# Expert down weights read in 16 KB pieces, and small parameters loaded as rows

## The chip, the cores and the metric

The kernel runs on one core of a Trainium2 chip. The metric is the device time of one execution in microseconds (us), as the median of several runs.

## The reference

The input is `x`, 256 tokens of 1024 float32 numbers. Two layers of the first block run in turn, then a final norm, then two layers of a second block:

```python
for l in range(2):
    x = x + hybrid_mixer(rmsnorm(x, norm_mix[l]), w_in[l], ...)          # attention and convolution
    x = x + hierarchical_moe(rmsnorm(x, norm_ffn[l]), router..., w_gate[l], w_up[l], w_down[l])
x = rmsnorm(x, norm_final)
# second block: swiglu (d_ff 2816), pool mixer, swiglu | swiglu, sparse attention, swiglu
def expert_block(xb, e):
    return (silu(xb @ w_gate[e]) * (xb @ w_up[e])) @ w_down[e]           # 32 experts per layer
```

An expert's gate and up weights are 1024 x 512 and its down weights 512 x 1024 float32, so each of the three is 2 MiB (2.097 MB), and the two layers read 64 experts x 3 x 2.097 MB = 403 MB of them. The small parameters are norm gains (vectors of 1024 or 512), convolution taps, attention sinks, router weights and biases, and the position tables of the sparse attention.

## The kernel before, in words

The stages run in the order mix0, moe0, mix1, moe1, final, ffn00, pool, ffn01, ffn10, nsa, ffn11. Each engine has an order written out by hand and waits on semaphores for the others.

**Weights.** All large weights are loaded by DMAs that the SP queue issues, each 2 MiB or less, into a ring of six slots (`ring`); in a MoE stage three more slots lie in `work` (`slot_of`), nine in all. A load is issued when the matmuls that used the slot's last content are done. The expert loads go pair by pair in the order gate, gate, up, up, down, down (`PAIR`, `moe_loads`; the issuing line is L530). The first nine loads of a MoE stage (`fill`) go out while the mixer before it still computes; the 87 that are left (`refill`) wait for PE to finish a gate, an up or a down product of an earlier pair. Gate and up weights are laid out so that partition `p` holds the rows `8p` to `8p+7`, 16 KB that lie together in memory; the down weights so that partition `p` holds the rows `p`, `p+128`, `p+256`, `p+384`, four pieces of 4 KB (`expert_src`).

**A pair of experts** (`one_pair` of the tensor engine): gate and up products (L905), the turn of the hidden activations `EB.h` by four 128 x 128 transposes (L943), the gather of the next pair's tokens (L892), the down product (L917), and the combination of the pair before (L926).

**Small parameters.** GpSimd issues all of them (`par`, L655), 7 for mix0 under one semaphore (`mix_param_loaded`) and 30 for the rest (`param_loaded`). The vectors are loaded in turned form, so that each 4-byte number is a piece of its own: element `k*128+p` goes to partition `p`. SP issues `x`, the constants table `cst` (identity and others), and the first two loads of `w_in`, then waits for the 7 parameter loads before it goes on. ScalarE and VectorE wait for the same 7 before they scale the turned `x` (L1395, L1826). PE turns `x` (L737), multiplies by `w_in` (L753 and L763) and later by `w_out` (L814). The mixer of layer 1 runs the same code.

Of the kernel before, what the change touches and what calls it, by code (L numbers as in the profile page):

```python
# [10 lines left out]
ALU = mybir.AluOpType  # L11
# [3 lines left out]
P = 128  # L15
SEQ, D = 256, 1024
TT = SEQ // P
KT = D // P
# [110 lines left out]
def build(nc, a, out, stages):  # L129
    ctx = ExitStack()  # L130
    with ctx:
# [30 lines left out]
        gT = sb("gT", [P, 10, KT])  # L162
        cw = sb("cw", [P, 2, 3, 4])
        gaT = sb("gaT", [P, 2, 4])
        gcT = sb("gcT", [P, 2, 4])
# [5 lines left out]
        cpos = sb("cpos", [P, 2, 16])  # L171
# [37 lines left out]
        S.mix_param_loaded = sem("mix_param_loaded")  # L209
# [73 lines left out]
        def expert_sems(tag, slots=RING):  # L283
# [17 lines left out]
            s.step = sem(f"step_{tag}")  # L301
            s.base_added = sem(f"base_added_{tag}")
# [4 lines left out]
        OV = {l: expert_sems(f"more{l}") for l in range(2) if f"moe{l}" in stages}  # L307

# [148 lines left out]
        FFN_GAIN = {"ffn00": 2, "ffn01": 3, "ffn10": 4, "ffn11": 6}  # L457
# [6 lines left out]
        MIX_PARAMS, PARAMS = 16 * 7, 16 * (8 + 6 + 2 + 6 + 1 + 2 + 1 + 4)  # L464
# [5 lines left out]
        def _(sp):  # L470
# [177 lines left out]
        N_PARAMS = [0, 0]  # L648

        @block.gpsimd  # L650
        def _(pool):
            w = Follow()

            def par(dst, src, first=False):
                pool.dma_start(dst, src).then_inc(S.mix_param_loaded if first else S.param_loaded, 16)  # L655
                N_PARAMS[0 if first else 1] += 16

            with nc.allow_non_contiguous_dma(reason="small parameters, transposed"):
                g2 = a["norm_gains_2"]
                def mixer_params(l):  # L660
                    for t in range(3):
                        par(cw[:, l, t, :], a["conv_w"][l, t].rearrange("(c p) -> p c", p=P), l == 0)
                    par(sink[:, l, :], a["attn_sink"][l].partition_broadcast(P), l == 0)
                    par(gcT[:, l, :], a["norm_conv_out"][l].rearrange("(c p) -> p c", p=P), l == 0)
                    par(gaT[:, l, :], a["norm_attn_out"][l].rearrange("(c p) -> p c", p=P), l == 0)
# [9 lines left out]
                mixer_params(1)  # L675
                par(gT[:, 1, :], a["norm_mix"][1].rearrange("(k p) -> p k", p=P))
                par(gT[:, 5, :], g2[1, 2].rearrange("(k p) -> p k", p=P))
                for n, src in ((2, g2[0, 0]), (3, g2[0, 4]), (4, g2[1, 0]), (6, g2[1, 4]), (7, g2[0, 2])):
                    par(gT[:, n, :], src.rearrange("(k p) -> p k", p=P))
# [3 lines left out]
                for s, name in enumerate(("nsa_cmp_pos_k_2", "nsa_cmp_pos_v_2")):  # L683
                    for r in range(2):
                        par(cpos[r * DH:(r + 1) * DH, s, :],
                            a[name][0].rearrange("(j r) d -> r d j", r=2)[r])
# [1718 lines left out]
```

## Time and profile before

| | us |
|---|---|
| median of 3 runs | 2221.74 |
| lowest and highest run | 2219.32, 2222.49 |
| the profiled execution's own time | 2221.96 |
| its span, first to last instruction | 2220.1 |
| PE busy in it | 2109.5 (95%) |
| VectorE busy | 775.1 (35%) |
| ScalarE busy | 631.8 (28%) |
| GpSimd busy | 35.7 (2%) |
| SP queue's packets, as a share of 16 DMA engines | 68.1% |

PE, PEld, DVE, ACT, POOL and SP are the tensor engine's matmuls and weight loads, VectorE, ScalarE, GpSimd and SyncE; a q behind a name is that engine's queue of instructions.

### The profile page before, as it was taken

How to read it: one execution, taken by the hardware profiler on the slowest of the kernel's cores; microseconds unless marked ns; L12 is line 12 of the kernel's file. 1: busy time of each engine (PE TensorE's matmuls, PEld its weight loads, DVE VectorE, ACT ScalarE, POOL GpSimd, SP SyncE). 2: the span in 40 equal slices, each digit the busy share in tenths (PEclk: the TensorE clock that was granted, in tenths of full speed). 3: DMA queues.
4: the chain of work that ended last, by engine and by line, in shares of the span. 5: the costliest groups of instructions: out<-in, count | busy, mean ns of one | idle time of the engine just before them, and what ended most of it. 6: DMA issues, size and time to landing. Idle time of an engine off the chain costs nothing.

```text
span 2220.1 us, 28261 instructions
## 1 busy us (share of the span) xinstructions
PE 2109.5 (95%) x11946; PEld 1427.5 (64%) x11946; DVE 775.1 (35%) x1151; ACT 631.8 (28%) x932; POOL 35.7 (2%) x53
## 2 busy tenths in 40 slices
PE   6999999999989999999998999899999999999998
PEld 4764444444467544444443999689989994667997
DVE  1431111111124311111112655465565542475555
ACT  1311111111123111111112433343343332373333
POOL 5000000000000000000000000000000000000000
PEclk9989999999999999999999999999999999999999
DMA  9449999999973599999999743464464454504530
GB/s 268 186 190 394 420 420 423 423 423 421 413 270 139 201 424 421 422 421 422 421 422 410 290 148 110 161 247 151 170 223 158 160 194 141 190 1 152 208 112 21
DMA packets 142467, 599.05 MB, mean 270 GB/s; under 512 B 6913, under 2 KB 22337, under 8 KB 126002
## 3 DMA queue, kind: packets, MB, share of 16 engines
q1 hardware_dynamic: 139730, 592.01, 68.1%
q0 software_dynamic: 2656, 5.86, 1.1%
q8 instruction: 63, 1.03, 0.2%
q14 instruction: 18, 0.15, 0.0%
HBM read 596.80 MB, written 1.05 MB: 269 GB/s over the span
## 4 chain that ended last, share of the span: by engine, by line
PE 76%; DMA 14%; DVE 4%; SPq 4%; ACT 1%; issue 1%; DVEq 0%; ACTq 0%
PE PS L1047 21%; PE PS L905 13%; PE PS L1061 10%; PE PS L917 6%; DMA work<-in_w_expert_up 5%; DMA ring<-in_w_expert_up 5%; PE PS L763 4%; SPq L530 4%; PE PS L892 3%; PE PS L1134 3%; PE PS L814 3%; PE PS L1034 2%; PE PS L753 2%; PE PS L926 2%; DMA work<-in_w_expert_down 1%; PE PS L1287 1%
## 5 line engine op out<-in xcount | busy, mean ns | idle before, releaser
L905 PE MATMUL PS<-ring,xs 128*64 128x512 f32 x1408 | 381.9, 598 | 16.1 <-DMA ring<-in_w_expert_up 16.1
L1315 ACT ACTIVATE split<-ring 128x2048 fp32r<-128x2048 f32 x132 | 253.2, 1921 | 425.9 <-PE PS L1047 268.0
L1792 DVE TENSOR_TENSOR split<-ring,split 128x2048 fp32r<-128x2048 f32 x132 | 302.4, 2293 | 178.0 <-ACT split L1315 172.9
L1047 PE MATMUL PS<-hT_high,split 128*128 128x256 f32 x2560 | 329.1, 281 | 0.0
L1047 PEld LDWEIGHTS PS<-hT_high,split 128*128 128x128 f32 x2560 | 316.5, 189 | 2.8
L905 PEld LDWEIGHTS PS<-ring,xs 128*64 128x64 f32 x1408 | 124.0, 138 | 219.7 <-issue 205.4
L1061 PE MATMUL PS<-split,ffn_hid 128*128 128x512 f32 x1056 | 246.9, 390 | 0.0
L905 PE MATMUL PS<-work,xs 128*64 128x512 f32 x640 | 217.2, 615 | 15.8 <-DMA work<-in_w_expert_up 15.8
L1061 PEld LDWEIGHTS PS<-split,ffn_hid 128*128 128x128 f32 x1056 | 195.5, 188 | 39.0
L1047 PE MATMUL PS<-hT_low,split 128*128 128x256 f32 x1280 | 178.3, 282 | 0.0
L1984 DVE TENSOR_TENSOR work<-PS,work 128x512 f32<-128x512 f32 x32 | 22.1, 691 | 410.9 <-PE PS L905 410.9
L1047 PEld LDWEIGHTS PS<-hT_low,split 128*128 128x128 f32 x1280 | 163.6, 189 | 0.0
L1990 DVE SCALAR_TENSOR_TENSOR y_low<-PS,work,y_high 128x512 fp32r<-128x512 f32 x64 | 48.0, 750 | 308.1 <-ACT y_high L1489 308.1
L905 PEld LDWEIGHTS PS<-work,xs 128*64 128x64 f32 x640 | 70.5, 142 | 111.3 <-issue 111.1
L917 PE MATMUL PS<-ring,work 128*64 128x512 f32 x640 | 141.7, 595 | 0.0
L1315 ACT ACTIVATE work<-PS 128x512 f32<-128x512 f32 (+1 forms) x65 | 40.0, 619 | 341.1 <-PE PS L943 295.9
L892 PE MATMUL PS<-work,hp 128*128 128x128 f32 x1024 | 124.2, 281 | 3.1 <-DVE work L1965 3.1
L892 PEld LDWEIGHTS PS<-work,hp 128*128 128x128 f32 x1024 | 121.4, 198 | 3.9 <-issue 3.9
L1489 ACT ACTIVATE y_high<-PS,work 128x512 fp32r<-128x512 f32 x64 | 44.0, 687 | 187.2 <-PE PS L917 187.2
L917 PEld LDWEIGHTS PS<-ring,work 128*64 128x64 f32 x640 | 44.2, 137 | 82.4 <-issue 80.0
L763 PE MATMUL PS<-hT,ring 128*128 128x256 f32 x384 | 87.3, 383 | 0.0
L917 PE MATMUL PS<-work 128*64 128x512 f32 x384 | 85.0, 595 | 0.9 <-DMA work<-in_w_expert_down 0.9
(287 smaller groups left out, 1851.2 us busy)
## 6 DMA issues: line engine op xcount, KB each, us to landing
ring<-in_w_expert_gate SPq DMA_DIRECT2D x44, 2048.0 KB, 24.4
ring<-in_w_expert_up SPq DMA_DIRECT2D x44, 2048.0 KB, 26.8
ring<-in_w_expert_down SPq DMA_DIRECT2D x40, 2048.0 KB, 31.5
work<-in_w_expert_down SPq DMA_DIRECT2D x24, 2048.0 KB, 30.2
work<-in_w_expert_gate SPq DMA_DIRECT2D x20, 2048.0 KB, 23.9
work<-in_w_expert_up SPq DMA_DIRECT2D x20, 2048.0 KB, 26.8
ring<-in_ffn_w_gate SPq DMA_DIRECT2D x20, 2048.0 KB, 8.6
ring<-in_ffn_w_up SPq DMA_DIRECT2D x20, 2048.0 KB, 8.9
```

The lines of the kernel that those rows point to most:

```text
L530: sp.dma_start(slot_of(r, 4 if which == "down" else KT), expert_src(l, 2 * pair + e, which)) \
L763: last = pe.matmul(PS[:, bank, (c % 2) * SEQ:(c % 2 + 1) * SEQ], wv[:, k, c * P:(c + 1) * P], hT[:, k, :], start=(k == 0), stop=(k == KT - 1))
L814: last = pe.matmul(PS[:, bank + h, :], src[:, c, t * P:(t + 1) * P], wv[:, c, h * 512:(h + 1) * 512], start=(c == 0), stop=(c == 3))
L892: last = pe.matmul(PS[:, 6 + b, (k % 4) * P:(k % 4 + 1) * P], hp[:, t, k * P:(k + 1) * P], EB.OH[:, t, :], start=(t == 0), stop=(t == 1))
L905: last = pe.matmul(PS[e * CAP:(e + 1) * CAP, bank, :], xs[:, k, e * CAP:(e + 1) * CAP], slot_of(slots[e], KT)[:, k, :], start=(k == 0), st ...
L917: last = pe.matmul(PS[e * CAP:(e + 1) * CAP, 6 + c, :], EB.hT[:, k, e * CAP:(e + 1) * CAP], slot_of(slots[e], 4)[:, k, c * 512:(c + 1) * 512],
L1047: last = pe.matmul(PS[:, bank, ft * SEQ:(ft + 1) * SEQ], split_cols(b, kind, part)[:, k, ft * P:(ft + 1) * P], hx[:, k, :], start=(n_ == 0 ...
L1061: last = pe.matmul(PS[:, 2 * t + c, :], ffn_hid[:, b % 2, hpart, ft, t * P:(t + 1) * P], wv[:, ft, c * 512:(c + 1) * 512], start=(b == 0 a ...
L1134: last = pe.matmul(PS[:, banks[t], offs[t]:offs[t] + width], hT[:, k, t * P:(t + 1) * P], wv[:, k, :], start=(k == 0), stop=(k == KT - 1))
L1315: return act.activation(o, i, ACT.Copy)
L1792: v.tensor_tensor(at[:, 1], src, at[:, 0], ALU.subtract).then_inc(S.ffn_low, 1)
L1990: v.scalar_tensor_tensor(y_low[:, c, :], PS[:, 6 + c, :], EB.gs[:, 0:1], y_high[:, c, :], ALU.mult, ALU.subtract).then_inc(s.y_made, 1)
```

## The change

1. `expert_src` lays the down weights out as `(p f) n -> p f n`: partition `p` reads the rows `4p` to `4p+3`, 16 KB in one piece. The hidden activations are turned to match: transpose `k` reads every fourth column of `EB.h`, from column `k`.
2. The gains, the convolution taps and the position tables are read as 152 rows of 128 numbers by 8 DMAs that ScalarE issues before its first stage, into a corner of `work` (`param_rows`). PE turns them by two transposes, and VectorE copies the 152 columns into one tile (`params`), of which `gT`, `cw`, `gaT`, `gcT`, `cpos` are now views.
3. GpSimd first loads one sink table, waits until the first two products with `w_in` are done (`projected` at 3), and only then issues its other 12 parameter loads.
4. SP loads `cst` before `x`, and its wait for the small parameters between the second and third load of `w_in` is gone.
5. Inside the MoE code VectorE counts its own steps with one semaphore where it had several, the numbering of the gains changes, and the branch for an expert with more than 64 tokens, which this input does not take, counts differently.

```diff
+        params = sb("params", [P, 152])
+        gT = params[:, 0:80].rearrange("p (n k) -> p n k", k=KT)
+        cw = params[:, 80:104].rearrange("p (l t c) -> p l t c", l=2, t=3)
...
+        param_rows = work[:, WORK - 2 * P:WORK].rearrange("p (a q) -> p a q", a=2)
...
                 if which == "down":
-                    return a["w_expert_down"][l, e].rearrange("(f p) n -> p f n", p=P)
+                    return a["w_expert_down"][l, e].rearrange("(p f) n -> p f n", f=4)
...
                 for lo, hi, k in ((0, 512, 2), (512, 768, 1), (1280, 1792, 2), (1792, 2304, 2), (768, 1280, 2)):
-                    if n[0] == 2:
-
-                        sp.wait_ge(S.mix_param_loaded, MIX_PARAMS)
                     wide(wi, lo, hi, S.projected, k, "(k p) n -> p k n")
...
+            sp.dma_start(cst[:, :], a["consts"]).then_inc(S.const_loaded, 16)
             sp.dma_start(x[:, :, :], a["x"][0].rearrange("(t p) d -> p t d", p=P)).then_inc(S.x_loaded, 16)
-            sp.dma_start(cst[:, :], a["consts"]).then_inc(S.const_loaded, 16)
...
-            with nc.allow_non_contiguous_dma(reason="small parameters, transposed"):
...
-                par(gT[:, 0, :], a["norm_mix"][0].rearrange("(k p) -> p k", p=P), True)
-                mixer_params(0)
+            pool.dma_start(sink[:, 0, :], a["attn_sink"][0].partition_broadcast(P)).then_inc(S.sink_loaded, 16)
+            pool.wait_ge(S.projected, 3)
+            with nc.allow_non_contiguous_dma(reason="small parameters"):
                 for l in range(2):
                     par(wr[:, l, :, 0:NG], a["w_router_group"][l].rearrange("(k p) n -> p k n", k=KT))
                     par(wr[:, l, :, NG:], a["w_router_expert"][l].rearrange("(k p) n -> p k n", k=KT))
-                    par(gT[:, 8 + l, :], a["norm_ffn"][l].rearrange("(k p) -> p k", p=P))
                     par(rbias[:, l, 0:NG], a["b_router_group"][l].partition_broadcast(P))
                     par(rbias[:, l, NG:], a["b_router_expert"][l].partition_broadcast(P))
...
             pool.wait_ge(S.param_loaded, PARAMS)
+            pool.wait_ge(S.rows_taken, 1)
...
                 transpose_x(f"mix{l}", 4)
+                pe.wait_ge(S.rows_taken, 1)
                 project(512, (0, 1), first=True)
...
                     for k in range(4):
-                        last = pe.transpose(PS[:, 4, k * P:(k + 1) * P], EB.h[:, k * P:(k + 1) * P], ident)
+                        last = pe.transpose(PS[:, 4, k * P:(k + 1) * P],
+                                            EB.h.rearrange("p (q k) -> p k q", k=4)[:, k, :], ident)
...
             pe.wait_ge(S.const_loaded, w.to(S.const_loaded, 16))
+            pe.wait_ge(S.rows_loaded, ROWS)
+            pe.transpose(PS[:, 0, 0:104], param_rows[0:104, 0, :], ident[0:104, 0:104])
+            pe.transpose(PS[:, 0, 104:152], param_rows[0:48, 1, :], ident[0:48, 0:48]).then_inc(S.rows_turned, 1)
             pe.wait_ge(S.set_up, w.to(S.set_up, 2))
...
                 if l == 0:
-                    act.wait_ge(S.mix_param_loaded, MIX_PARAMS)
+                    act.wait_ge(S.rows_taken, 1)
...
+            g2 = a["norm_gains_2"]
+            for dst, src in ((param_rows[0:16, 0, :], a["norm_mix"].rearrange("l (k p) -> (l k) p", p=P)),
+                             (param_rows[16:64, 0, :], g2.rearrange("i (j b) (k p) -> b (i j) k p", b=2, p=P)[0]),
+                             (param_rows[64:80, 0, :], a["norm_ffn"].rearrange("l (k p) -> (l k) p", p=P)),
+                             (param_rows[80:104, 0, :], a["conv_w"].rearrange("l t (c p) -> (l t c) p", p=P)),
+                             (param_rows[0:8, 1, :], a["norm_attn_out"].rearrange("l (c p) -> (l c) p", p=P)),
+                             (param_rows[8:16, 1, :], a["norm_conv_out"].rearrange("l (c p) -> (l c) p", p=P)),
+                             (param_rows[16:32, 1, :], a["nsa_cmp_pos_k_2"][0].rearrange("(j r) d -> j (r d)", r=2)),
+                             (param_rows[32:48, 1, :], a["nsa_cmp_pos_v_2"][0].rearrange("(j r) d -> j (r d)", r=2))):
+                act.dma_start(dst, src).then_inc(S.rows_loaded, 16)
...
                 if l == 0:
-                    v.wait_ge(S.mix_param_loaded, MIX_PARAMS)
+                    v.wait_ge(S.sink_loaded, 16)
...
             v.memset(epsb[:, :], EPS).then_inc(S.set_up, 1)
-            v.wait_ge(S.x_loaded, w.to(S.x_loaded, 16))
             v.wait_ge(S.const_loaded, w.to(S.const_loaded, 16))
             v.tensor_copy(ident_r[:, :], ident)
             v.tensor_copy(causal_r[:, :], const("causal")).then_inc(S.set_up, 1)
+            v.wait_ge(S.rows_turned, w.to(S.rows_turned))
+            v.tensor_copy(params[:, :], PS[:, 0, 0:152]).then_inc(S.rows_taken, 1)
+            v.wait_ge(S.rows_taken, w.to(S.rows_taken))
+            v.wait_ge(S.x_loaded, w.to(S.x_loaded, 16))
```

## Rows read from the trace of the kernel before

**Rows 1.** The page: busy tenths and GB/s of 40 slices of 55.5 us.

```profile
DMA  9449999999973599999999743464464454504530
GB/s 268 186 190 394 420 420 423 423 423 421 413 270 139 201 424 421 422 421 422 421 422 410 290 148 110 161 247 151 170 223 158 160 194 141 190 1 152 208 112 21
```

**Rows 2.** The chain that ended last: start us, us, what.

```profile
1.75 19.79 DMA ring<-in_w_in
...
140.00 5.35 PE PS L994 x24
...
214.37 13.73 PE PS L905 x64
...
241.41 13.73 PE PS L905 x64
...
446.02 7.11 PE PS L905 x32
...
505.75 8.49 PE PS L905 x32
...
574.12 31.09 DMA work<-in_w_expert_down
...
1193.54 21.57 DMA ring<-in_ffn_w_up
```

**Rows 3.** Stretches: us, busy us (instructions) per engine, granted clock, DMA share, GB/s.

```profile
397.00:412.00 15.00, 15.00 (x84) 6.91 (x84) 2.48 (x7) 3.85 (x5) 0.00 (x0) 1.00 1.01 428
...
416.50:423.50 7.00, 7.00 (x26) 2.58 (x24) 0.00 (x0) 0.00 (x0) 0.00 (x0) 0.76 1.02 407
...
810.00:1180.00 370.00, 354.89 (x1832) 163.59 (x1830) 49.91 (x117) 65.11 (x91) 0.00 (x0) 0.99 1.01 422
```

**Rows 4.** Packets of 397 to 412 us, then of 416.5 to 423.5 us.

```profile
DMA packets 440, 6.42 MB, mean 428 GB/s; under 512 B 48, under 2 KB 48, under 8 KB 48
...
DMA packets 712, 2.85 MB, mean 407 GB/s; under 512 B 16, under 2 KB 16, under 8 KB 712
```

**Rows 5.** First 50 us in order: start us, us, instruction [idle before <-releaser].

```profile
0.76 0.44 SPq L613 DMA_DIRECT2D x<-in_x  x1
...
2.04 0.20 ACT L1353 ACTIVATE small<-epsb 128x1 f32<-128x1 f32 x1
...
8.50 3.65 PE L737 MATMUL PS<-cst,x 128*128 128x128 f32 x16 [8.50 <-DVE causal_r L2356]
...
12.50 1.57 ACT L1395 ACTIVATE hT<-PS,gT 128x256 f32<-128x256 f32 x4 [2.85 <-DMA gaT<-in_norm_attn_out]
...
21.59 23.75 PE L753 MATMUL PS<-ring,hT 128*128 128x512 f32 x64 [9.44 <-DMA ring<-in_w_in]
```

**Rows 6.** DMA traffic and issues of the first 30 us; KB each, us to landing.

```profile
GB/s 0 0 87 153 360 360 382 413 370 199 180 143 191 237 292 226 251 259 153 241 292 200 183 167 115 179 245 215 260 249 185 132 138 144 189 243 210 202 179 189
DMA packets 4102, 6.31 MB, mean 210 GB/s; under 512 B 896, under 2 KB 1984, under 8 KB 4102
...
x<-in_x SPq DMA_DIRECT2D x1, 1024.0 KB, 5.2
...
gaT<-in_norm_attn_out POOLq DMA_DIRECT2D x2, 2.0 KB, 6.7
```

**Rows 7.** In order of time, layer 0 ends and layer 1 begins.

```profile
603.14 0.60 PE L943 MATMUL PS<-cst,work 128*128 128x128 f32 x4
...
605.35 7.09 PE L917 MATMUL PS<-work 128*64 128x512 f32 x32 [0.47 <-DMA work<-in_w_expert_down]
...
621.21 3.64 PE L737 MATMUL PS<-cst,x 128*128 128x128 f32 x16 [6.00 <-issue]
...
624.69 20.88 PE L753 MATMUL PS<-ring,hT 128*128 128x512 f32 x64
```

**Rows 8.** Stretches behind x's transposes, columns as in rows 3.

```profile
624.80:631.80 7.00, 7.00 (x18) 3.17 (x18) 2.01 (x11) 1.87 (x5) 0.00 (x0) 1.00 1.04 394
...
1451.00:1458.00 7.00, 7.00 (x49) 7.00 (x49) 6.89 (x17) 3.62 (x6) 0.00 (x0) 0.78 0.85 340
```

More of the change, by code:

```diff
@@ L208, in build @@
         S.x_loaded = sem("x_loaded")
-        S.mix_param_loaded = sem("mix_param_loaded")
+        S.rows_loaded = sem("rows_loaded")
+        S.rows_turned = sem("rows_turned")
+        S.rows_taken = sem("rows_taken")
+        S.sink_loaded = sem("sink_loaded")
         S.param_loaded = sem("param_loaded")
@@ L307, in build @@
         OV = {l: expert_sems(f"more{l}") for l in range(2) if f"moe{l}" in stages}
+        for l in OV:
+            OV[l].step = sem(f"step_more{l}")
         def mixer_views():
@@ L455, in half_of @@
             return src[:, :, (b % 2) * BLOCK:(b % 2 + 1) * BLOCK], r
-        FFN_GAIN = {"ffn00": 2, "ffn01": 3, "ffn10": 4, "ffn11": 6}
+        FFN_GAIN = {"ffn00": 2, "ffn01": 4, "ffn10": 5, "ffn11": 7}
         def first_slot(stage):
             return sum(LOADS[name[:3]] for name in stages[:stages.index(stage)])
-        MIX_PARAMS, PARAMS = 16 * 7, 16 * (8 + 6 + 2 + 6 + 1 + 2 + 1 + 4)
+        ROWS, PARAMS = 16 * 8, 16 * 12
         block = ctx.enter_context(nc.Block())
@@ L647, in build @@
         gains = gain_list()
-        N_PARAMS = [0, 0]
+        N_PARAMS = [0]
         @block.gpsimd
@@ L652, in _, with par @@
             w = Follow()
-            def par(dst, src, first=False):
-                pool.dma_start(dst, src).then_inc(S.mix_param_loaded if first else S.param_loaded, 16)
-                N_PARAMS[0 if first else 1] += 16
-            with nc.allow_non_contiguous_dma(reason="small parameters, transposed"):
[L659 to L665, printed above, removed]
-                par(gT[:, 0, :], a["norm_mix"][0].rearrange("(k p) -> p k", p=P), True)
-                mixer_params(0)
+            def par(dst, src):
+                pool.dma_start(dst, src).then_inc(S.param_loaded, 16)
+                N_PARAMS[0] += 16
+            pool.dma_start(sink[:, 0, :], a["attn_sink"][0].partition_broadcast(P)).then_inc(S.sink_loaded, 16)
+            pool.wait_ge(S.projected, 3)
+            with nc.allow_non_contiguous_dma(reason="small parameters"):
                 for l in range(2):
@@ L671, in _ @@
                     par(wr[:, l, :, NG:], a["w_router_expert"][l].rearrange("(k p) n -> p k n", k=KT))
-                    par(gT[:, 8 + l, :], a["norm_ffn"][l].rearrange("(k p) -> p k", p=P))
                     par(rbias[:, l, 0:NG], a["b_router_group"][l].partition_broadcast(P))
                     par(rbias[:, l, NG:], a["b_router_expert"][l].partition_broadcast(P))
[L675 to L679, printed above, removed]
+                par(sink[:, 1, :], a["attn_sink"][1].partition_broadcast(P))
                 for h in range(2):
@@ L1012, in moe @@
                 with pe.If(most > CAP):
-                    pe.wait_ge(OV[l].base_added, 1)
+                    pe.wait_ge(OV[l].step, TT)
                     experts(OV[l], Follow(), MORE * PAIRS, y_high[l], lambda p: [(n[0] + j) % RING for j in range(6)])
@@ L1599, in nsa @@
                         i = act.activation(hT[:, 2 * b + k, :], PS[:, 4 + b, k * SEQ:(k + 1) * SEQ], ACT.Copy,
-                                           scale=gT[:, 5, 2 * b + k:2 * b + k + 1])
+                                           scale=gT[:, 6, 2 * b + k:2 * b + k + 1])
                     i.then_inc(S.hT_even, 1)
@@ L1959, in experts @@
             def experts(s, f, passes, pos, gate, y_high):
-                f.step = s.step
                 iota = const("iota").unsqueeze(1).to_broadcast([P, 2, CAP])
@@ L2094, in moe @@
                 experts(M, w, PAIRS, B.pos, B.gate, y_high[l])
-                w.step = S.dve_step
                 most = v.value_load(flag[0:1, l:l + 1], min_val=0, max_val=SEQ)
@@ L2099, in moe @@
                         v.wait_ge(M.combined, w.after(M.combined, t + 1))
-                        add_experts(t).then_inc(OV[l].base_added if t else OV[l].step, 1)
-                    v.wait_ge(OV[l].base_added, 1)
+                        add_experts(t).then_inc(OV[l].step, 1)
                     f = Follow(OV[l].step)
-                    v.wait_ge(f.step, f.to(f.step))
+                    v.wait_ge(f.step, f.to(f.step, TT))
                     v.memset(B.gatev[:, :, MORE * NE:], 0.0).then_inc(f.step, 1)
```

22 lines of the change are left out of this document (7 added, 15 removed).

## The prediction

> **What bounds the kernel now.** I first read the page's rows of DMA share and rate [rows 1]. It splits the run into two kinds of stretch. In slices 4 to 11 and 15 to 22 (about 170 to 610 us and 780 to 1220 us, the two MoE stages) the DMA engines are busy 90% or more, at 394 to 424 GB/s. From ffn00 on the share is mostly 30 to 60%. The 95% of PE in the table of times therefore says little about the MoE stages. The chain of waits tells them apart [rows 2]. While the nine slots are still full, the pair of gate and up products starts every 27.04 us (214.37, 241.41): that is PE's own pace. Later the chain alternates between a DMA and a product, and the up product that waited comes at 446.02 and two pairs on at 505.75, so every 29.87 us: that is the pace at which 12.58 MB arrive at some 422 GB/s [rows 3]. Layer 0's MoE ends on a down load that lands at 605.2 (574.12 + 31.09), and the stage that follows moe1 begins on a load of ffn00 that is queued behind the experts' (1193.54, 21.57 us) [rows 2]. So in both MoE stages what ends last is the stream of bytes. It is saturated from slice 4 on, when the first refills go out, to the stage's end [rows 1].
>
> Next the first 22 us. The chain opens with one DMA, the first `w_in` load, issued at 1.75 and landed at 21.54 [rows 2]. The turned `x` was ready long before: PE's transposes ran from 8.50 to 12.15, ScalarE began to scale at 12.50 after it had waited for the last of the seven small loads, and PE then stood for 9.44 us for `w_in` [rows 5]. The traffic says why 2.1 MB took 20 us: after about 6.7 us the rate falls from 360 to 413 GB/s to mostly 115 to 290, and 896 of the 4102 packets of the first 30 us are below 512 bytes [rows 6]. Those are the turned parameters.
>
> **Down weights in one piece.** A stretch of down loads alone shows it. From 397 to 412 us only gate and up weights move, 440 packets for 6.42 MB with 48 small ones, so (6.42 MB by 392) 16 KB each; from 416.5 to 423.5 only down weights, 2.85 MB in 696 pieces, 4 KB each [rows 4]. The DMA share is full in both; the rates are 428 and 407 GB/s [rows 3]. A load of 2.097 MB takes 4.900 us at 428 and 5.153 at 407, a difference of 0.253 us. The long average, 422 GB/s over 810 to 1180 us [rows 3], gives a second value: all at 428 would save 1 - 422/428 = 1.40% of the time of the saturated bytes. Each layer has 32 down loads; the two of pair 0 are among the nine fills that PE doesn't wait for, so 30 refills count, 60 in all. By the first value that is 60 x 0.253 = 15.2 us. By the second, 2 x 87 refills x 2.097 MB = 364.9 MB take 864.7 us at 422 and 852.5 at 428: 12.1 us. I take 13.2, a little nearer to the long average, as 7 us is a short sample; the bounds are 12.1 and 15.2. All of it is on the path, because a down at the end of the stream pays for all the loads before it. PE does not take over: its 27.04 us a pair stay below 6 x 4.90 = 29.4.
>
> The Trainium skill says otherwise for this part: "DMA: Bandwidth & Descriptors", section Specifications, asks for at least 512 B in a transfer to reach line rate. By that rule 4 KB pieces already run at line rate and the part brings 0 of the 13.2 us; this case's rows differ (407 against 428).
>
> **Turning h by every fourth column.** Four transposes per pair now read with a step of four numbers. The four took 0.60 us [rows 7]. No row shows such a read by PE. The nearest is the same kind of transpose in the starting microseconds, 16 in 3.65 us [rows 5], 0.23 us each against 0.60 / 4 = 0.15 here: so the bounds are 0 and, taking a full doubling, +0.6 us a pair. In the middle of a stage this is hidden under PE's waits for the DMAs (29.4 - 27.0 = 2.4 us a pair). Only the last pair of a layer can show it: its down product waited 0.47 us for its weights [rows 7], and with two faster loads between the last up and the last down (2 x 0.25 = 0.5) PE and DMA get there together. So the cover is gone exactly there: 0 to 1.2 us for both layers. I take 0.2, near the end of no change, because nothing in the rows speaks for a full doubling.
>
> **The start.** SP now issues `cst`, `x` and all five `w_in` loads without a wait; 30 parameter loads leave these microseconds. Two paths meet in the first product with `w_in`.
> Path one is `w_in`. `x` and `cst` are 1.05 and 0.40 MB, the first load 2.10 MB; 3.54 MB at 377 GB/s, the mean of the five undisturbed slices (360 to 413) [rows 6], take 9.4 us. The traffic starts in the third slice of 0.75 us, at about 2.2 us, and `x` landed at 5.96 (0.76 + 5.2) [rows 6], 1.0 us later than its 2.8 us at this rate. 2.2 + 9.4 + 1.0 = 12.6 us.
> Path two is the parameters. ScalarE is free at 2.24 [rows 5]. Eight issues by SP's price, 0.44 us [rows 5], end at 5.8. The rows are 78 KB. A load in an empty queue begins to move about 1.5 us after its issue (0.76 to 2.2 for `x`); with sharing I allow 3.2 us to landing, so 9.0; the bound above is the 6.7 us of a small load of before [rows 6], 12.5. Then two transposes on PE (0.5 us) at 9.5. The 16 transposes of `x` are queued behind them on PE, as are all later products: 9.5 + 3.65 = 13.2. `x` has landed at 8. VectorE's copy of 152 columns (about 0.3 us) and the scaling run beside PE's transposes. So the first product starts at 13.2 instead of 21.59: 8.4 us earlier; bounds 9.0 (if `w_in` at 12.6 sets it) and 4.9 (rows at 12.5).
> The products then run faster too. The same 64 take 23.75 us in layer 0 [rows 5] and 20.88 in layer 1 [rows 7]; layer 1's ran at the full 2.4 GHz right behind the transposes (clock 1.00) [rows 8], while layer 0's came after 9.4 us of idleness. With the gap closed layer 0 should be like layer 1, 2.9 us. But ffn00's successor, ffn01, shows a mean clock of 0.78 for 7 us behind such transposes [rows 8], so (1 - 0.78) x 7 = 1.5 us may stay lost. I take 2.2, with 0 and 2.9 as bounds. From then on layer 0 is a chain of PE work and its `w_in` loads come early enough (the other four, 7.3 MB, are in by about 32 us; the third is first needed some 21 us after the start). What follows, the nine fills and the first refill included, is released by PE and moves with it.
> GpSimd's 12 loads now go out at about 33 us, when `projected` is 3. Behind that wait stand the router weights, the bias tables and the two gain rows. At up to 0.9 us each with 6.7 to land they are in by some 52 us; the router product that wants them (L994) is at 140 [rows 2], some 129 after the gain. Its cover is over 70 us: cost nothing. The step counting, the numbering and the untaken branch cost nothing: they are waits on instructions long done, or not run.
>
> **Sum.** 13.2 + 8.4 + 2.2 - 0.2 = 23.6 us. The profiled execution took 1.86 us more than its span of 2220.1, and that stays: 2221.96 - 23.6 = 2198.4; against the median, 2221.74 - 23.6 = 2198.1. I predict 2198.1 us. With all bounds on one side it is 2221.7 - (15.2 + 9.0 + 2.9) = 2194.6, on the other 2221.7 - (12.1 + 4.9 - 1.2) = 2205.9.
>
> **Rivals.**
> *The pieces don't matter (chance 0.07).* The down stretches are slower for another reason than their length, say the order of the rows in memory. Against it: gate and up loads have the very shape that the down loads get. Then only the start counts: 2221.7 - 10.6 + 0.2 = 2211.3. The Trainium skill's 512 B rule above would give this result.
> *The start doesn't come (0.10).* ScalarE's eight issues are held up, or the rows land late because they share the engines with `x` and `w_in`: if the rows land 8.4 us later than I have them (17.4 us), nothing is gained there and 2221.7 - 13.0 = 2208.7 follows. For it: no row shows ScalarE issuing a load, nor two hardware queues at once. Against it: the rows are 152 pieces of 512 B instead of thousands of 4 B.
> *Slower (0.03).* The strided transposes make PE the bound of the MoE stages. Its place is L943. At S us more per pair PE alone needs 27.04 + S. From the third pair's first product (214.37) [rows 2] to the end of layer 0's last down product (605.35 + 7.09) [rows 7] are 398.1 us, against 14 x 27.04 = 378.6: 19.5 us of cover in a layer. The loss outweighs the start's 10.6 us when 2 x (14 S - 19.5) exceeds it: S above 1.77 us, 0.44 a transpose, which would be four times as long as now. At S = 2.5 it is 2221.7 - 10.6 + 31 = 2242. "SBUF — State Buffer", section Door 1 (the Trainium skill), says SBUF is read in lines of 16 bytes and each step to a new line costs; a step of four float32 numbers is just that. No row here shows such a read.
> *Forecast (0.77)*; the 0.03 that is left lies around it, half on each side.
>
> **Range.** The likeliest case alone spans 2194 to 2206. To reach 8 in 10 with the second rival in, I give 2193 to 2209. This kernel's runs tell 0.2% (4.4 us) from no change. Faster than that: the forecast and the first two rivals, 0.94. Slower 0.03, the same 0.03.
>
> **What would show it.** The down loads alone move at 428 GB/s and no 4 KB packet is left in 397 to 412 or anywhere in the experts' stream; the pace of the waiting up products is near 29.4 us; L943 lasts about as long as now. The first L753 starts near 13 us, its wait is gone or below 1 us, and its group takes near 21 us. ffn00 begins some 23 us earlier, and everything behind it has the same length. The prediction fails if the first L753 still waits for `w_in` or for the rows, if the rate of the down stretches stays at 407, or if PE's pace per pair rises above 29 us.

## The result, and the profile after

| | before | after |
|---|---|---|
| median, us | 2220.53 (4 runs) | 2196.88 (4 runs) |
| lowest and highest run | 2217.98, 2222.49 | 2193.85, 2199.19 |
| ratio of after to before, 95% interval | | 0.9898 [0.9886, 0.9909] |
| the profiled execution and its span | 2221.96, 2220.1 | 2196.52, 2194.7 |

The change makes the kernel 23.65 us faster by the medians (20.2 to 25.3 by the interval); the forecast was 23.6. The gain comes in two kinds of place, the start and the two streams of expert weights, as the prediction said. Inside the start the first product gained 2.1 us less than forecast and the clock 0.6 us more. That the total fits to 0.05 us is luck, as the part on why the prediction was right works out.

Line numbers moved: L905 is now L892 (gate and up products), L917 L904 (down), L943 L930 (the turn of h), L737 L723 (the turn of x), L753 L739, L763 L749, L814 L800; in the ffn stages L1034 is L1022, L1047 L1035 and L1061 L1049, in nsa L1188 is L1176 and L1261 is L1249.

The page of after, its rows of DMA share and rate and its count of packets, against [rows 1]; the last line is before's count:

```profile
DMA  9359999999954599999999552554365353504630
GB/s 348 149 197 428 428 429 427 429 429 428 410 213 192 237 429 428 427 429 428 428 429 405 206 192 80 222 206 173 115 239 203 109 213 120 192 1 154 220 106 19
DMA packets 117373, 599.05 MB, mean 273 GB/s; under 512 B 6243, under 2 KB 21819, under 8 KB 92716
```

```profile
DMA packets 142467, 599.05 MB, mean 270 GB/s; under 512 B 6913, under 2 KB 22337, under 8 KB 126002
```

The inner slices of both MoE stages read 427 to 429 GB/s where they read 420 to 424, and the first slice 348 instead of 268. Of the 25094 packets that are gone 24576 are the down weights' (64 loads x 384).

The DMA view of after from 810 to 1140 us, inside moe1, and the windows of the same stretch and of three others (us, busy us and instructions of PE, PEld, DVE, ACT and POOL, granted clock, DMA share, GB/s), against [rows 3, 4]:

```profile
DMA packets 9705, 141.30 MB, mean 428 GB/s; under 512 B 1081, under 2 KB 1081, under 8 KB 1081
```

```profile
810.00:1140.00 330.00, 319.76 (x1655) 146.76 (x1655) 44.67 (x105) 59.96 (x83) 0.00 (x0) 0.99 1.01 428
722.00:740.00 18.00, 14.84 (x91) 12.07 (x92) 12.01 (x50) 4.49 (x10) 0.00 (x0) 0.91 0.17 71
1889.00:1910.00 21.00, 18.86 (x143) 15.31 (x143) 8.84 (x22) 6.06 (x15) 0.00 (x0) 0.83 0.82 302
577.00:587.00 10.00, 9.35 (x35) 3.70 (x36) 0.43 (x1) 0.00 (x0) 0.00 (x0) 0.83 0.99 412
```

The whole mix of gate, up and down loads now moves at 428, the rate that gate and up loads alone had before. Every packet under 8 KB in it is also under 512 bytes, so none of 4 KB is left.

The start of after in order of time (start us, us, instruction, idle before and its releaser), against [rows 5]:

```profile
0.76 0.40 SPq L615 DMA_DIRECT2D cst<-in_consts  x1
1.21 1.36 ACTq L1699 DMA_DIRECT2D work<-in_norm_gains  x1
1.68 17.14 SPq L490 DMA_DIRECT2D ring<-in_w_in  x5
4.69 0.49 ACTq L1699 DMA_DIRECT2D work<-in_nsa_cmp_pos_v  x1
11.18 0.41 PE L1281 MATMUL PS<-cst,work 104*128 104x104 f32 x1 [11.18 <-DMA work<-in_nsa_cmp_pos_v]
11.79 3.67 PE L723 MATMUL PS<-cst,x 128*128 128x128 f32 x16
15.29 20.91 PE L739 MATMUL PS<-ring,hT 128*128 128x512 f32 x64
36.52 0.91 POOL L657 DMA_DIRECT2D wr<-in_w_router_group  x1 [34.59 <-PE PS L739]
```

The first product starts at 15.29, without any wait behind the transposes of x, where before it stood 9.44 us for `w_in` and came at 21.59.

The chain that ended last in after (start us, us, what), against [rows 2]:

```profile
4.69 6.35 DMA work<-in_nsa_cmp_pos_v
11.18 0.41 PE PS L1281
...
176.57 13.73 PE PS L892 x64
203.71 13.73 PE PS L892 x64
...
401.40 7.09 PE PS L892 x32
...
460.17 7.09 PE PS L892 x32
...
546.21 31.31 DMA ring<-in_w_expert_up
577.65 8.78 PE PS L892 x32
...
589.23 7.04 PE PS L904 x32
```

PE's own pace is 27.14 us a pair (27.04 before); the up products that wait come every 29.4 us (460.17 - 401.40, halved) instead of 29.87. Layer 0 ends on its last up load; the last down product no longer waits.

Where the 25.4 us between the two profiled executions arise, by the start of the same instruction in both (the last column is what is new in that stretch):

| instruction | before | after | ahead by | new |
|---|---|---|---|---|
| first product with `w_in` | 21.59 | 15.29 | 6.3 | 6.3 |
| end of its group of 64 | 45.34 | 36.20 | 9.1 | 2.8 |
| first gate product of moe0 | 161.10 | 150.24 | 10.9 | 1.7 |
| last up product of moe0 | 595.09 | 577.65 | 17.4 | 6.6 |
| last down product of moe0 | 605.35 | 589.16 | 16.2 | -1.2 |
| first product of mix1 | 624.85 | 608.72 | 16.1 | -0.1 |
| first gate product of moe1 | 759.62 | 738.64 | 21.0 | 4.9 |
| last up product of moe1 | 1194.15 | 1166.82 | 27.3 | 6.4 |
| first product of ffn00 | 1232.89 | 1205.17 | 27.7 | 0.4 |
| nsa, L1188 and L1176 | 1917.83 | 1889.11 | 28.7 | 1.0 |
| last work | 2201.47 | 2176.08 | 25.4 | -3.3 |

The two starts give 6.3 + 2.8, the two streams 6.6 + 6.4. The others are stretches whose work is nearly the same: there the granted clock differs between the two executions. Two stretches of before, columns as above:

```profile
740.00:758.00 18.00, 15.06 (x69) 13.41 (x70) 11.05 (x47) 2.33 (x6) 0.00 (x0) 0.72 0.14 60
1917.80:1938.80 21.00, 18.10 (x157) 14.76 (x158) 11.16 (x29) 7.25 (x22) 0.00 (x0) 0.92 0.84 307
```

The router of layer 1 reads 0.91 (the window 722 to 740 above) where before had 0.72 (0.78 from 743 to 761, the window aligned by the first gate product). The last up product of moe0 took 8.78 us instead of 7.09, in a window that reads 0.83 (before's product: 1.00). At nsa's start 0.83 stands against 0.92, and from there to the end 3.3 us go back.

### The profile page after: what moved, and what is told of

Same layout as the page of the kernel before. It is cut to its first block, busy times and chain, and to the rows that moved or that the text cites. A ratio compares the mean times of both kernels' runs of the same rounds, so it can differ in the third digit from the quotient of the medians.

```text
span 2194.7 us, 28252 instructions
## 1 busy us (share of the span) xinstructions
PE 2103.1 (96%) x11948; PEld 1425.0 (65%) x11948; DVE 775.8 (35%) x1152; ACT 631.7 (29%) x932; POOL 16.2 (1%) x29
## 4 chain that ended last, share of the span: by engine, by line
PE 83%; DMA 11%; DVE 4%; ACT 1%; issue 1%; ACTq 0%; SPq 0%; DVEq 0%
PE PS L1035 21%; PE PS L892 16%; PE PS L1049 10%; PE PS L904 8%; DMA ring<-in_w_expert_up 7%; PE PS L879 4%; PE PS L749 4%; PE PS L1122 3%; DMA work<-in_w_expert_up 3%; PE PS L800 3%; PE PS L1022 2%; PE PS L913 2%; PE PS L739 2%; PE PS L1275 1%; DMA ring<-in_ffn_w_up 1%; PE PS L723 1%
## 5 line engine op out<-in xcount | busy, mean ns | idle before, releaser
L892 PE MATMUL PS<-ring,xs 128*64 128x512 f32 x1408 | 383.5, 601 | 13.6 <-DMA ring<-in_w_expert_up 13.6
L1035 PE MATMUL PS<-hT_high,split 128*128 128x256 f32 x2560 | 329.1, 281 | 0.0
L1035 PEld LDWEIGHTS PS<-hT_high,split 128*128 128x128 f32 x2560 | 316.5, 189 | 2.8
L892 PEld LDWEIGHTS PS<-ring,xs 128*64 128x64 f32 x1408 | 124.9, 138 | 217.9 <-issue 207.8
L1049 PE MATMUL PS<-split,ffn_hid 128*128 128x512 f32 x1056 | 246.9, 390 | 0.0
L1049 PEld LDWEIGHTS PS<-split,ffn_hid 128*128 128x128 f32 x1056 | 195.5, 188 | 39.0
L892 PE MATMUL PS<-work,xs 128*64 128x512 f32 x640 | 213.5, 604 | 6.8 <-DMA work<-in_w_expert_up 6.8
L1035 PE MATMUL PS<-hT_low,split 128*128 128x256 f32 x1280 | 178.3, 282 | 0.0
L1035 PEld LDWEIGHTS PS<-hT_low,split 128*128 128x128 f32 x1280 | 163.6, 189 | 0.0
L1984 DVE TENSOR_TENSOR work<-PS,work 128x512 f32<-128x512 f32 x32 | 22.1, 692 | 397.2 <-PE PS L892 397.2
L904 PE MATMUL PS<-ring,work 128*64 128x512 f32 x640 | 141.7, 595 | 0.0
L892 PEld LDWEIGHTS PS<-work,xs 128*64 128x64 f32 x640 | 69.3, 139 | 100.0 <-issue 99.8
L904 PEld LDWEIGHTS PS<-ring,work 128*64 128x64 f32 x640 | 44.1, 137 | 82.4 <-issue 80.0
L749 PE MATMUL PS<-hT,ring 128*128 128x256 f32 x384 | 87.3, 383 | 0.0
L904 PE MATMUL PS<-work 128*64 128x512 f32 x384 | 85.0, 595 | 0.0
## 6 DMA issues: line engine op xcount, KB each, us to landing
ring<-in_w_expert_up SPq DMA_DIRECT2D x44, 2048.0 KB, 24.4
```

The lines of the kernel that those rows point to most:

```text
L749: last = pe.matmul(PS[:, bank, (c % 2) * SEQ:(c % 2 + 1) * SEQ], wv[:, k, c * P:(c + 1) * P], hT[:, k, :], start=(k == 0), stop=(k == KT - 1))
L892: last = pe.matmul(PS[e * CAP:(e + 1) * CAP, bank, :], xs[:, k, e * CAP:(e + 1) * CAP], slot_of(slots[e], KT)[:, k, :], start=(k == 0), st ...
L904: last = pe.matmul(PS[e * CAP:(e + 1) * CAP, 6 + c, :], EB.hT[:, k, e * CAP:(e + 1) * CAP], slot_of(slots[e], 4)[:, k, c * 512:(c + 1) * 512],
L1035: last = pe.matmul(PS[:, bank, ft * SEQ:(ft + 1) * SEQ], split_cols(b, kind, part)[:, k, ft * P:(ft + 1) * P], hx[:, k, :], start=(n_ == 0 ...
L1049: last = pe.matmul(PS[:, 2 * t + c, :], ffn_hid[:, b % 2, hpart, ft, t * P:(t + 1) * P], wv[:, ft, c * 512:(c + 1) * 512], start=(b == 0 a ...
```

## The experiments

All times are medians in us, ratios are to the kernel before on the same chip, with 95% intervals. Where a gain or loss is given with an interval it is the ratio's; the difference of the medians can be a few us off it. The kernel before gave 2218.8, 2218.5 and 2218.9 in the three groups of runs. The change itself, repeated:

> The changed kernel once more, as the yardstick of this call: 2194 to 2199 us.

Measured 2194.01, ratio 0.9888 [0.987, 0.9906], 24.9 us faster. The result stands.

**The two halves apart.** `down_only` is the kernel before with part 1 of the change alone:

```diff
-                    return a["w_expert_down"][l, e].rearrange("(f p) n -> p f n", p=P)
+                    return a["w_expert_down"][l, e].rearrange("(p f) n -> p f n", f=4)
...
-                        last = pe.transpose(PS[:, 4, k * P:(k + 1) * P], EB.h[:, k * P:(k + 1) * P], ident)
+                        last = pe.transpose(PS[:, 4, k * P:(k + 1) * P],
+                                            EB.h.rearrange("p (q k) -> p k q", k=4)[:, k, :], ident)
```

> The kernel before with part 1 alone: down weights in 16 KB pieces and the h columns taken by fours; the small parameters stay as they were. Theory (the length of the pieces sets the rate of a down load, and all 60 refilled down loads are on the path): 12 to 15 us less than before, about 2207 us; the DMA stream at 428 GB/s throughout; the first L753 still waits some 9 us for w_in. Rival (the down loads are slow for another reason): within 2 us of before.

Measured 2204.26, ratio 0.9926 [0.9902, 0.995]: 16.4 us faster (11 to 22), 14.6 by the medians. From 810 to 1140 us it moves 428 GB/s, like the whole change, and its first product still comes at 22.32 behind `w_in`.

`rows_only` is the kernel after with those two edits taken back:

> The changed kernel with part 1 undone: down weights in four 4 KB pieces, h turned by blocks; the small parameters as rows. Theory: the start is worth 9.1 us (6.3 earlier, 2.8 of faster products), so about 2211 us; with down_only the two parts add up to the whole, 23.7 us. Rival (what the start gains is given back in the saturated stages, whose stream doesn't begin earlier): less than 4 us below before.

Measured 2209.49, ratio 0.9961 [0.9945, 0.9976]: 8.7 us faster (5 to 12), 9.3 by the medians. Its first group of 64 products is like after's, and the rate from 810 to 1140 us is before's, 422 GB/s. 16.4 + 8.7 = 25.1 (23.9 by the medians) against 23.65 and 24.9 for the whole: the halves add up, within intervals of several us.

**Length or order of the pieces?** The new layout changes the length of a piece and also which rows a partition holds. `near4k` keeps the rows, and so the memory that a partition reads, and stores the four of them in reverse order, so that no two pieces can be joined:

```diff
+                    dst = dst[:, ::-1, :] if which == "down" else dst
...
-                    sp.dma_start(slot_of(r, 4 if which == "down" else KT), expert_src(l, 2 * pair + e, which)) \
+                    to = slot_of(r, 4 if which == "down" else KT)
+                    to = to[:, ::-1, :] if which == "down" else to
+                    sp.dma_start(to, expert_src(l, 2 * pair + e, which)) \
...
-                                            EB.h.rearrange("p (q k) -> p k q", k=4)[:, k, :], ident)
+                                            EB.h.rearrange("p (q k) -> p k q", k=4)[:, 3 - k, :], ident)
```

> The changed kernel, but each partition's four rows are stored in reverse order, so that the 16 KB that lie together in memory are moved in four pieces of 4 KB; the transposes of h take the columns to match. Theory (length of the piece): the down stretches run at 407 to 410 GB/s again and the kernel is 12 to 15 us slower than the changed one, about 2210 us. Rival (where the rows lie in memory decides, not the length): 428 GB/s and the time of the changed kernel.

Measured 2208.62, ratio 0.9947 [0.9931, 0.9964], by the ratios 11 us above after. The same memory, in 4 KB pieces, is slow again. That the reversed order is not what costs is shown by the kernel before and rows_only, whose 4 KB pieces are stored in rising order and which move the same 422 GB/s over this stretch.

`piece8k` gives a partition two pieces of 8 KB:

```diff
-                    return a["w_expert_down"][l, e].rearrange("(p f) n -> p f n", f=4)
+                    return a["w_expert_down"][l, e].rearrange("(g p f) n -> p g f n", g=2, f=2)
...
-                                            EB.h.rearrange("p (q k) -> p k q", k=4)[:, k, :], ident)
+                                            EB.h.rearrange("p (g q f) -> p g f q", g=2, f=2)[:, k // 2, k % 2, :], ident)
```

> The changed kernel with down loads in two pieces of 8 KB per partition. Theory with a fixed cost per piece (worked out from the rates of 16 KB and 4 KB pieces, 4.90 and 5.13 us a load: 128 and 512 pieces over 16 engines, so some 9.5 ns a piece and engine): 4.97 us a load, 60 x 0.076 = 4.6 us slower than the changed kernel, about 2201.5 us. Rival (a step somewhere between, no cost per piece): either the time of the changed kernel or 13 us more.

Measured 2202.24, ratio 0.9921 [0.9905, 0.9938].

`piece2k` reverses eight pieces of 2 KB, and the down product takes them in that order:

```diff
-                    return a["w_expert_down"][l, e].rearrange("(p f) n -> p f n", f=4)
+                    return a["w_expert_down"][l, e].rearrange("(p f) (c n) -> p (f c) n", f=4, c=2)
...
+                    dst = dst[:, ::-1, :] if which == "down" else dst
...
-                                                 slot_of(slots[e], 4)[:, k, c * 512:(c + 1) * 512],
+                                                 slot_of(slots[e], KT)[:, 7 - (2 * k + c), :],
```

> The changed kernel with down loads in eight pieces of 2 KB per partition, stored in reverse order. Theory with some 9.5 ns a piece and engine: 1024 pieces, 5.43 us a load instead of 4.90, 60 x 0.53 = 32 us slower than the changed kernel, about 2229 us, down stretches near 386 GB/s. Rival (pieces below 4 KB cost no more): 12 to 15 us slower, as with 4 KB.

Measured 2226.74, ratio 1.0042 [1.0027, 1.0056]: slower than the kernel before. The DMA views from 810 to 1140 us of near4k, piece8k and piece2k:

```profile
DMA packets 18000, 139.17 MB, mean 422 GB/s; under 512 B 1058, under 2 KB 1058, under 8 KB 12322
```

```profile
DMA packets 12507, 140.52 MB, mean 426 GB/s; under 512 B 1072, under 2 KB 1072, under 8 KB 1072
```

```profile
DMA packets 28789, 136.36 MB, mean 413 GB/s; under 512 B 1040, under 2 KB 1040, under 8 KB 23242
```

A third of the bytes are down weights. If m is the mean rate of the stretch and r that of the down loads, then 3/m = 2/428 + 1/r. This gives:

| piece | pieces a load | m, GB/s | r, GB/s | us a load |
|---|---|---|---|---|
| 16 KB | 128 | 428 | 428 | 4.90 |
| 8 KB | 256 | 426 | 422 | 4.97 |
| 4 KB | 512 | 422 | 410 | 5.11 |
| 2 KB | 1024 | 413 | 386 | 5.43 |

From 128 to 1024 pieces a load costs 0.53 us more, over 896 pieces on 16 engines: some 9.5 ns a piece on its engine, and the two steps between follow it (0.08 and 0.23 by it, 0.07 and 0.21 read). Each rate is read to half a GB/s, which is some 0.02 us of a load. The times agree: by the ratios piece8k, near4k and piece2k are 5, 11 and 32 us above after, each known to some 3 us, where the table gives 60 loads x 0.07, 0.21 and 0.53 = 4, 13 and 32. Length decides, and the price is one per piece. How the engine spends the 9.5 ns no run shows. The Trainium skill, "DMA: Bandwidth & Descriptors", section Specifications, gives line rate from 512 B on; the runs disagree, with 386, 410 and 422 GB/s at 2, 4 and 8 KB against 428.

**The strided turn.** `contig_turn` is the kernel after with the old transposes, so the activations meet the wrong rows of the down weights and the experts' outputs are other numbers:

```diff
-                        last = pe.transpose(PS[:, 4, k * P:(k + 1) * P],
-                                            EB.h.rearrange("p (q k) -> p k q", k=4)[:, k, :], ident)
+                        last = pe.transpose(PS[:, 4, k * P:(k + 1) * P],
+                                            EB.h[:, k * P:(k + 1) * P], ident)
```

> The changed kernel, but h is turned by blocks of 128 columns again, while the down weights keep their new layout, so each activation meets the wrong row of the down weights. Theory: the strided read lengthens the four transposes by some 0.1 us a pair in all, hidden under the waits for the DMAs: time within 1 us of the changed kernel, the weight loads of the transposes back from 0.21 to 0.14 us each. Rival (the strided read is on the path): 2 us or more faster than the changed kernel.

Measured 2192.86, ratio 0.9881 [0.9864, 0.9897], inside the spread of the single executions of the change (2190.26 to 2199.19). Its interval and theirs overlap, so a cost of the stride on the whole is not seen. By itself it is seen. The instructions of L930 in after, then in contig_turn (ns min/median/max):

```profile
L930 PEld LDWEIGHTS PS<-cst,work x128: 196/212/224, 165.0 to 1175.1; 128*128 128x128 f32 x128
L930 PE MATMUL PS<-cst,work x128: 283/285/388, 165.0 to 1175.3; 128*128 128x128 f32 x128
```

```profile
L930 PEld LDWEIGHTS PS<-cst,work x128: 137/140/147, 165.1 to 1181.8; 128*128 128x128 f32 x128
L930 PE MATMUL PS<-cst,work x128: 269/273/328, 165.1 to 1181.9; 128*128 128x128 f32 x128
```

The strided operand of a transpose is the one that is loaded as weights: 0.21 us instead of 0.14, four times a pair. That is the direction that the Trainium skill gives ("SBUF — State Buffer", section Door 1: each step to a new line of 16 bytes costs), here with 1.5 times the load. PE's pace a pair is 27.14 us with the stride and 27.03 in contig_turn, both far below the 29.4 of the DMAs.

**GpSimd's loads.** `pool_early` is the kernel after without the wait of part 3, so its 12 loads go out at once, and behind them two more, which stand after the same wait in GpSimd's order: the first two gain rows (`gB`), each copied to all 128 partitions, 512 KB a load:

```diff
-            pool.wait_ge(S.projected, 3)
```

> The changed kernel without GpSimd's wait for the first two products with w_in: its 12 parameter loads go out in the first microseconds. Theory (small pieces in the first microseconds delay w_in): the first L739 waits for w_in and starts 1 to 4 us later than 15.3. Rival (w_in is early enough either way, the rows set the start): L739 starts at 15.3 +- 0.5.

One execution: 2206.97, span 2205.2, some 10 us above after. The chain of waits of pool_early:

```profile
1.68 22.70 DMA ring<-in_w_in
...
24.47 23.33 PE PS L738 x64
```

The first product comes 9.2 us later than in after, and 2.9 later than in the kernel before. The expectation was far too small: fourteen loads from GpSimd's queue hold the first `w_in` load up to 24.38, and the gain of the first product's start hangs on the wait for `projected`. Both bytes and small pieces are in it, and this run doesn't part them. Up to 24.4 us 6.52 MB moved, 1.59 MB of them GpSimd's, at a mean of 267 GB/s; in after 3.96 MB moved up to 14.2 us, at 279. In between, from 8 to 13 us, the rate is 104 to 216 GB/s, where before has 143 to 292 [rows 6]; it falls before the two gain rows are issued at 10.3.

**ScalarE's loads.** The first 15 us of after show a dip of the traffic between about 5.6 and 6.8 us (40 slices of 0.375 us):

```profile
GB/s 0 0 0 0 58 145 140 313 392 399 350 415 393 393 273 30 45 51 147 216 321 348 392 396 402 412 393 408 371 393 382 377 410 363 385 371 358 358 350 350
```

My theory was that ScalarE's eight issues hold SP's queue up. `rows_late` issues them only when x has landed:

```diff
+            act.wait_ge(S.x_loaded, 16)
             g2 = a["norm_gains_2"]
```

> The changed kernel, but ScalarE issues its 8 row loads only once x has landed. In the changed kernel the traffic falls to 30 to 50 GB/s between 5.3 and 6.8 us. Theory (ScalarE's eight issues hold up what SP's queue hands to the DMA engines): the gap is gone, the first w_in load lands near 12.3 us instead of 14.2, but the rows land near 14 and the products start later, at 17 to 19 us. Rival (the gap belongs to SP's own queue): the gap stays at the same place and w_in lands at 14.

One execution: 2205.43, span 2203.6. The first 15 us of rows_late:

```profile
GB/s 0 0 0 0 66 173 198 321 356 410 371 371 437 360 228 23 66 131 213 279 322 399 393 404 415 404 410 410 426 393 404 374 374 385 365 350 340 336 346 328
```

The dip stays, a little narrower, the first `w_in` load lands at 13.8 instead of 14.2, and the theory falls. Where the dip comes from stays open: the rival put it in SP's own queue, but before issues `x`, `cst` and `w_in` from the same queue and shows none at this place (361 to 412 GB/s). The first product came at 21.41, behind rows that landed at 17.17, so this run also shows half of the rival "the start doesn't come": with late rows the first product is where it was before. Its group was fast all the same, 20.88 us, and ended 3.1 us earlier than before's.

**The order on PE.** In after PE turns the parameter rows first and x second. `x_first` swaps them:

```diff
                 transpose_x(f"mix{l}", 4)
+                if l == 0:
+                    pe.wait_ge(S.rows_loaded, ROWS)
+                    pe.transpose(PS[:, 0, 0:104], param_rows[0:104, 0, :], ident[0:104, 0:104])
+                    pe.transpose(PS[:, 0, 104:152], param_rows[0:48, 1, :], ident[0:48, 0:48]).then_inc(S.rows_turned, 1)
...
-            pe.wait_ge(S.rows_loaded, ROWS)
-            pe.transpose(PS[:, 0, 0:104], param_rows[0:104, 0, :], ident[0:104, 0:104])
-            pe.transpose(PS[:, 0, 104:152], param_rows[0:48, 1, :], ident[0:48, 0:48]).then_inc(S.rows_turned, 1)
```

> The changed kernel, but PE turns x before it turns the parameter rows. The rows landed at 11.0 us, x at 8.6, the first w_in load at 14.2. Theory (the rows, and PE's transposes of x queued behind them, set the start): x is turned while the rows are awaited and the first L739 group starts at 14.0 to 14.4 instead of 15.3, now set by w_in; about 1 us less than the changed kernel, near what five rounds can tell. Rival (something else sets the start): still 15.3.

Measured 2193.09, ratio 0.9874 [0.9857, 0.989], like again's 2194.01 beside it. The chain of waits of x_first, then of again:

```profile
1.68 12.38 DMA ring<-in_w_in
14.14 23.86 PE PS L739 x64
```

```profile
15.63 20.97 PE PS L739 x64
```

The product comes 1.5 us earlier, as intended, and its group ends 1.4 us later (38.00 against 36.60), in these two traces. The traced execution of x_first took 2201.31 us, 8 us or more above its three others, so the medians don't bear this loss out; the trace shows what can happen. Between the transposes and `w_in` PE now idles for 1.42 us. The instructions of the first 6 us of each group (ns min/median/max), in x_first, again and the kernel before:

```profile
L739 PE MATMUL PS<-ring,hT x7: 972/1057/1191, 14.1 to 19.4; 128*128 128x512 f32 x7
```

```profile
L739 PE MATMUL PS<-ring,hT x13: 592/592/942, 15.5 to 21.0; 128*128 128x512 f32 x13
```

```profile
L753 PE MATMUL PS<-ring,hT x8: 593/1061/1222, 21.6 to 27.5; 128*128 128x512 f32 x8
```

The same product takes 1.06 us behind a gap of 1.42 or 9.44 us and 0.59 us behind transposes without a gap, and 7 or 8 products start in these 6 us against 13. I read this as the lower and the higher of TensorE's two levels, 1.2 and 2.4 GHz. The mean of granted clock reads 1.00 in all three stretches and doesn't show it, so the level is inferred from the durations.

The other traces bear out the difference and not its exact size. By the rows in order of time, nine groups without a gap ahead last 20.8 to 22.0 us, 21.2 on the mean (after, again, rows_only, near4k, piece8k, piece2k, contig_turn, rows_late, before_busy49). Five behind a gap of 1.42 to 10.98 us last 22.8 to 23.9, 23.5 on the mean (x_first, before_busy, pool_early, before, down_only). That is 2.2 us. And near4k's first four products have a median of 0.95 us with no gap ahead of them, so a gap is not all that decides it; what else does stays open.

**A busy PE in the kernel before.** To test the term for the clock alone, the kernel before gets products without use behind the transposes of x, first 28, then 49:

```diff
                 transpose_x(f"mix{l}", 4)
+                if l == 0:
+                    keep_clock(28)
```

> The kernel before, with 28 products of the identity on PE behind the transposes of x in mixer 0, while w_in is awaited (their result is overwritten). Theory (the 2.9 us by which layer 0's first products are slower are the clock, after 9.4 us of idleness): the group L753 takes 20.9 us instead of 23.75, and the kernel gains 2.5 to 3 us. Rival (the products are slow because they are the first ones, or because of the traffic): still 23.75 us.

Measured 2219.57, ratio 0.9999 [0.9986, 1.0011]. Inconclusive for the kernel's time: the 28 took only 6.71 us, PE then idled for 4.98 us until `w_in` was there, and the group took 23.63 us as before.

> The kernel before with 49 instead of 28 products of the identity behind the transposes of x. The 28 took 6.7 us and ended 5.0 us before w_in landed, and L753 was slow again; 49 should last until about 22 us. Theory (idleness ahead of the products costs the clock): the group L753 takes 20.9 us instead of 23.75, 2 to 3 us gained, less what the 49 overshoot. Rival (the first products are slow whatever PE did before): 23.7 us.

Measured 2215.75, ratio 0.999 [0.9977, 1.0004]: the median is 3.1 us lower, but no change lies inside the interval. The chain of waits of before_busy49:

```profile
12.21 12.32 PE PS L985 x49
24.52 20.64 PE PS L753 x64
```

The 49 cover the gap and the group takes 20.64 us instead of 23.75, with the same products and the same loads in flight. So most of the difference comes from what PE did just before, and not from these products being the first. But the 49 run past the landing of `w_in`, the group starts 2.9 us late and ends at 45.16 against 45.34: in the traces no time is won.

## Why the prediction was right, point by point

- **Down weights in one piece, 13.2 (12.1 to 15.2): right.** The streams gave 6.6 + 6.4 = 13.0 in the traces. By the rates it is 60 x (5.11 - 4.90) = 12.6; down_only alone gave 16.4 (11 to 22; 14.6 by the medians). That length and not order decides, and with it the fall of the first rival, rests on near4k, piece8k and piece2k. The long average was the better of the two samples: the 407 GB/s of 7 us would have given 15.2.
- **The strided turn, -0.2 (0 to 1.2): the place was wrong, the size harmless.** It costs 4 x 0.07 us of weight loads, 0.1 us of pace a pair. I had the last down product of a layer pay for it; it no longer waits at all, because the last up load ends the layer. The four turns stand between that up product and the down product, so the cost is on the path once in a layer, some 0.1 us. The rival with S above 1.77 us a pair is far off.
- **The first product, 8.4 (4.9 to 9.0): mis-sized, 6.3.** The step that failed is the landing of the rows: 9.0 predicted, 11.04 measured. The eight issues ended at 5.18, near my 5.8; the last load took 6.35 us from issue to landing, near the 6.7 of a small load in [rows 6], which I had kept as a bound only, and not the 3.2 that I allowed from the end of the issues (it took 5.9 from there). The form of the path was right: rows, two transposes, 16 transposes, first product with no wait. `w_in` landed at 14.2, not 12.6; the dip of the traffic from 5.6 to 6.8 us had no term in my sum. It would have set 14.2 at best, as x_first shows.
- **The clock of the first products, 2.2 (0 to 2.9): right, 2.8 in this pair of traces, 2.2 on the mean of all.** The group took 20.91 us, as layer 1's had in before. before_busy49 and x_first show the mechanism from both sides, each in one trace. I took 2.2 out of a doubt from ffn01; that the mean of 14 traces is 2.2 as well is luck, since no trace ties the two.
- **GpSimd's late loads at nothing: right** for the wait itself, which is hidden as forecast. What I had not seen is what the wait is worth: pool_early, in its one execution, is about 10 us above after, with 14 loads behind the wait and not the 12 that I counted.
- **ffn00 some 23 us earlier and all behind it of the same length: wrong in the detail.** It began 27.7 us earlier and the end came 25.4 earlier. The surplus comes from stretches with the same instructions at another granted clock (+1.7, -1.2, +4.9, +1.0, -3.3). Why the chip granted more or less in each of them stays open; the medians, 23.65 and 24.9 us apart, do not depend on one execution.

So 13.0 + 6.3 + 2.8 = 22.1 us are shown in place of 23.6. The start was forecast at 10.6 and gave 9.1. The 1.5 us between 22.1 and the 23.65 by the medians belong to no term; they are within what the interval leaves open (20.2 to 25.3). The mechanisms were right, but a hit to 0.05 us is luck.

## What to carry to other kernels

Where a stream of weights sets the time, count pieces, not only bytes. With about 9.5 ns a piece on its engine, as here, going from 4 to 16 KB pieces wins 4% of the load, and a layout of a contraction's rows is free to choose as long as the other operand is turned the same way. At the start of a kernel, load small vectors as rows and turn them on PE, and hold every load that nobody needs yet behind the first large one. When a change removes a wait of PE, look at what follows it too: the gap costs its own length and then, in all five traces with a gap here, slow products behind it.

## What the hardware showed unexpectedly

- Fourteen loads from GpSimd's queue in the first microseconds, 1.6 MB in all, put the landing of a 2.1 MB load from 14.2 to 24.4 us (after against pool_early).
- Behind an idle time of only 1.42 us the group of first products took 23.86 us instead of 20.97, as long as behind one of 9.44 us (23.75), while the mean of granted clock read 1.00 (one trace each).
- With fewer pieces SP's queue stops blocking. The gate loads issued from 140 to 600 us, first of before and then of after (ns min/median/max of an issue):

```profile
L530 SPq DMA_DIRECT2D ring<-in_w_expert_gate x19: 345/1493/18896, 175.6 to 561.5; - x19
```

```profile
L535 SPq DMA_DIRECT2D ring<-in_w_expert_gate x19: 328/333/434, 164.7 to 539.3; - x19
```

An issue took up to 18.9 us with 4 KB pieces in the queue and at most 0.43 us with 16 KB ones. SP's queue has 4% of the chain that ended last in before and 0% in after, so these waits are a rival for the cost of short pieces. Against it stand two readings. The DMA share is 1.01 from 810 to 1140 us in both kernels, so the engines don't run dry. And in piece8k no issue of a gate load took more than 0.47 us and SP has 0% of the chain, yet its load costs 0.07 us more than with 16 KB. So at 8 KB the price is not SP's waiting; at 4 and 2 KB, where the same price per piece fits, that is argued and was not tried by itself.
